# A hybrid decoder block on one core: each mixing program projects the first columns of the next

## The reference

```python
h = rmsnorm(x, mix_norm)
hq, hf, hi, hg, rq, rk, rv, rg, ga, gb = split(h @ w_in)   # 512 x4, 512, 512, 1024, 1024, 1024, 1024
ya = hgrn2_mix(hq, hf, hi, hg, lb, hg_norm)       # 4 heads of 128, chunks of 64
yb = retention_mix(rq, rk, rv, rg, pos, ret_norm) # 4 heads, keys 128, values 256, chunks of 128, rotary
#   in both: o = rmsnorm(per head) * silu(gate)
merged = sigmoid(ga) * (ya @ w_a) + sigmoid(gb) * (yb @ w_b)
x = x + merged @ w_out
x = x + hier_moe(rmsnorm(x))                      # 32 experts, top 1 group, top 2 in it
x = x + sigmoid(rmsnorm(x) @ w_ple_gate) * (p @ w_ple_proj)
return rmsnorm(x)
```

## Time and profile before

| | |
|---|---|
| median of 3 runs | 1540.79 us (1540.4 to 1540.8) |
| the profiled execution | 1540.26 us, its span 1538.4 us |
| PE busy | 1446.3 us, 94% of the span |
| DVE, ACT, POOL busy | 772.2 (50%), 592.4 (39%), 88.6 (6%) us |
| mean granted PE clock | 0.971 of 2.4 GHz |
| DMA | mean 133 GB/s |

### The profile page before, as it was taken

One profiled execution on the slowest core, in us unless ns is written; L12 is line 12 of the kernel. 1 busy time (PEld: TensorE's weight loads), 2 busy tenths in 40 slices (PEclk: granted clock), 3 DMA queues, 4 the chain that ended last, 5 costly groups with the idle time before them and its releaser, 6 DMA issues.

```text
span 1538.4 us, 19246 instructions
## 1 busy us (share of the span) xinstructions
PE 1446.3 (94%) x7882; PEld 1205.3 (78%) x7882; DVE 772.2 (50%) x953; ACT 592.4 (39%) x720; POOL 88.6 (6%) x75
## 2 busy tenths in 40 slices
PE   6999999878997999799999999999699999998997
PEld 5888778667885788588888888988588888876886
DVE  5410366633445543412222224326699999888664
ACT  5310222111112422211111113134488888887555
POOL 0000000000000000000000000000222222221000
PEclk9999999879998999999999999999699999999999
DMA  6200210022213111122222223722699999996221
GB/s 234 83 1 0 61 29 23 7 69 55 55 28 76 35 42 41 43 62 62 61 61 61 61 61 133 265 96 85 259 384 383 391 386 392 375 366 235 107 99 66
DMA packets 103805, 205.23 MB, mean 133 GB/s; under 512 B 12976, under 2 KB 73008, under 8 KB 90160
## 3 DMA queue, kind: packets, MB, share of 16 engines
q1 hardware_dynamic: 93184, 182.89, 33.9%
q0 software_dynamic: 9248, 16.80, 2.9%
q10 hardware_dynamic: 1296, 4.46, 0.7%
HBM read 187.86 MB, written 28.84 MB: 141 GB/s over the span
## 4 chain that ended last, share of the span: by engine, by line
PE 50%; DMA 3%; DVE 2%; ACT 1%; issue 1%; POOLq 0%; DVEq 0%; ACTq 0%; SPq 0%
PE two_banks L174 8%; PE two_banks L176 8%; PE two_banks L175 8%; PE two_banks L2443 4%; PE two_banks L2445 3%; PE two_banks L2444 3%; PE two_banks L2326 2%; PE two_banks L2572 2%; PE two_banks L2328 2%; PE two_banks L2327 2%; PE two_banks L2573 2%; PE two_banks L2574 2%; DMA two_chunk_raw<-w_e 2%; PE two_banks L2433 1%; PE two_banks L2362 1%
## 5 line engine op out<-in xcount | busy, mean ns | idle before, releaser
L1249 DVE TENSOR_TENSOR two_chunk_lo<-two_chunk_raw,two_hi 128x2048 fp32r<-128x2048 f32 x96 | 217.4, 2287 | 24.1 <-ACT two_hi L1245 23.1
L1245 ACT CAST two_hi<-two_chunk_raw 128x2048 fp32r<-128x2048 f32 x96 | 181.4, 1918 | 12.1 <-DMA two_chunk_raw<-w_e 11.7
L221 DVE TENSOR_TENSOR mix_w_lo<-mix_w_raw,mix_w_hi 128x1024 fp32r<-128x1024 f32 (+1 forms) x58 | 66.9, 1160 | 177.7 <-ACT mix_w_hi L217 177.7
L174 PE MATMUL two_banks<-mix_hT_hi,mix_w_hi 128*128 128x512 f32 x256 | 100.5, 392 | 9.9 <-DVE mix_w_lo L221 9.9
L2443 PE MATMUL two_banks<-two_hi,two_xT_hi 128*128 128x512 f32 x256 | 103.3, 404 | 2.3 <-DVE two_xT_lo L1633 1.7
L2445 PE MATMUL two_banks<-two_hi,two_xT_lo 128*128 128x512 f32 x256 | 100.6, 393 | 0.0
L2444 PE MATMUL two_banks<-two_chunk_lo,two_xT_hi 128*128 128x512 f32 x256 | 100.4, 392 | 0.0
L175 PE MATMUL two_banks<-mix_hT_lo,mix_w_hi 128*128 128x512 f32 x256 | 100.3, 392 | 0.0
L176 PE MATMUL two_banks<-mix_hT_hi,mix_w_lo 128*128 128x512 f32 x256 | 100.3, 392 | 0.0
L217 ACT CAST mix_w_hi<-mix_w_raw 128x1024 fp32r<-128x1024 f32 (+1 forms) x58 | 56.8, 985 | 96.4 <-PE two_banks L176 93.2
L174 PE MATMUL gate_gates<-mix_hT_hi,mix_w_hi 128*128 128x512 f32 x192 | 76.4, 398 | 4.9 <-DVE mix_w_lo L221 4.9
(11 more groups left out here) (306 smaller groups left out, 3215.4 us busy)
## 6 DMA issues: line engine op xcount, KB each, us to landing
two_chunk_raw<-w_e SPq DMA_DIRECT2D x102, 1024.0 KB
mix_w_raw<-w_in SPq DMA_DIRECT2D x44, 512.0 KB, 3.8
two_r<-results SPq DMA_DIRECT2D x16, 512.0 KB, 4.5
vals_w_raw<-w_in SPq DMA_DIRECT2D x12, 512.0 KB, 8.2
heads_values<-x SPq DMA_DIRECT2D x8, 512.0 KB, 11.0
reten_swapped<-reten_raw SPq DMA_DIRECT2D x8, 512.0 KB
mix_w_raw<-w_b SPq DMA_DIRECT2D x8, 512.0 KB, 4.7
two_x<-x SPq DMA_DIRECT2D x8, 512.0 KB, 7.5
```

What stands on the lines that cost most here:

```text
L174: nc.tensor.matmul(out, sh, mh, start=(k == 0), stop=False)
L1245: self.nc.scalar.copy(self.high(n)[:], self.raw(n)[:]).then_inc(self.hi_ok, 1)
L1249: self.nc.vector.tensor_tensor(self.low(n)[:], self.raw(n)[:], self.high(n)[:].bitcast(F32), ALU.subtract).then_inc(self.lo_ok, 1)
```

## The change

Each program now also projects the first columns of the one that follows, so that its last head has projections in it as the others do.

- HGRN head 3 projects retention head 0 (eight pieces), into the PSUM tile `sums` that all programs now share; its own outputs go to the tile of the pairs. ACT and DVE split the weights of retention head 1 at its end.
- The retention program begins with the copies of head 0 and the projection of head 1, of which three halves stand ahead of the first transposes. Its ring is numbered from head 1 on. Its last head projects gates 0 and 1 and splits the weights of gates 2 and 3. PE reads the values in place, and GpSimd's copy is gone.
- The squares and sums are taken in the retention: in each head those of two row tiles of the HGRN outputs, and from head 1 on those of the retention head before. The last head's are left to the gate program, in t = 0 and 1, with their own root after t = 2.
- The gate program keeps two gates ahead: turn t, projection t + 2. Projections 12 and 13 are ga and gb of merge tile 0. All loops are written out. ACT's order is silu(t), y_hi(t), high split t + 4.
- The merge starts tile 0 with its branch products.

The diff, cut to its core:

```diff
+            ring.load(sp, HG_HEADS, 0, w_in[:, :, RK:RK + RET_DK])
+            ring.load(sp, HG_HEADS, 1, w_in[:, :, RQ:RQ + RET_DK])
+            ring.ask(sp, 2 * HG_HEADS + 2, first_weights(dram, "reten"), kept["asked"]["reten"])
...
+            def retention_hi(u):
+                act.wait_ge(kept["asked"]["reten"][u], 16)
+                act.wait_ge(projected, 2 * HG_HEADS + u + 1)
+                nc.scalar.copy(ring.hi[:, u], ring.raw[:, u]).then_inc(kept["reten_split"][0], 1)
...
+            def retention_lo(u):
+                dve.wait_ge(kept["reten_split"][0], u + 1)
+                nc.vector.tensor_tensor(ring.lo[:, u], ring.raw[:, u], ring.hi[:, u].bitcast(F32),
+                                        ALU.subtract).then_inc(kept["reten_split"][1], 1)
...
-                    elif i:
-                        pe.wait_ge(out_stored, 2 * i)
-                    pe.wait_ge(state_ok, SU * i + 7)
+                    pe.wait_ge(state_ok, SU * i + 8)
...
-                    if i + 1 < HG_HEADS and n < 8:
+                    if n < 8:
...
+        def parts_of(i):
+
+
+            parts = [(values[:, t, 0:HG_W], mean[:, t, 0:HG_HEADS], HG_DV) for t in range(SUMS * i, SUMS * i + SUMS)]
+            if i:
+                col = HG_W + (i - 1) * RET_DV
+                parts += [(values[:, 2 * g:2 * g + 2, col:col + RET_DV], mean[:, 2 * g:2 * g + 2, HG_HEADS + i - 1], RET_DV)
+                          for g in range(4)]
+            return parts
...
-                if not at(i, RET_HEADS - 1):
-                    ring.load(sp, i + 1, 0, w_in[:, :, bass.ds(RQ + P + i * RET_DK, P)])
-                    ring.load(sp, i + 1, 1, w_in[:, :, bass.ds(RK + P + i * RET_DK, P)])
+                if i + 2 == RET_HEADS:
+                    ring.load(sp, i + 1, 0, w_in[:, :, HGATE:HGATE + P])
+                    ring.load(sp, i + 1, 1, w_in[:, :, HGATE + P:HGATE + 2 * P])
+                if i + 2 < RET_HEADS:
+                    ring.load(sp, i + 1, 0, w_in[:, :, RQ + (i + 2) * RET_DK:RQ + (i + 3) * RET_DK])
+                    ring.load(sp, i + 1, 1, w_in[:, :, RK + (i + 2) * RET_DK:RK + (i + 3) * RET_DK])
                 sp.wait_ge(copied, 2 * i + 2)
-                if not first(i):
+                if i:
                     sp.wait_ge(rot_ok, 2 * i)
...
+                for n, (src, _, _) in enumerate(parts_of(i), parts_before(i)):
+                    if n >= 2:
+                        act.wait_ge(reduced, n - 1)
+                    if n == parts_before(i) + SUMS:
+                        act.wait_ge(out_stored, 4 * i)
+                    to = sq[:, n % 2, :]
+                    nc.scalar.activation(to if len(src.shape) == 2 else to.rearrange("p (t c) -> p t c", t=2), src,
+                                         ACT.Square).then_inc(squared, 1)
                 keys(0)
                 keys(1)
                 for u in range(2):
                     if i + 1 < RET_HEADS:
                         copies(i + 1, u)
-                    if i + 2 < RET_HEADS:
-                        ring.split_hi(act, i + 2, u)
+                        if i + 2 <= RET_HEADS:
+                            ring.split_hi(act, i + 1, u)
+                    else:
+                        act.wait_ge(kept["asked"]["gate"][u], 16)
+                        act.wait_ge(projected, 2 * RET_HEADS - 1 + u)
+                        nc.scalar.copy(ring.hi[:, u], ring.raw[:, u]).then_inc(kept["gate_split"][0], 1)
+                if i + 1 == RET_HEADS:
+                    act.wait_ge(means, 2)
+                    nc.scalar.activation(root[:], mean[:], ACT.Sqrt).then_inc(rooted, 1)
...
+                def reduce():
+                    for n, (_, to, width) in enumerate(parts_of(i), parts_before(i)):
+                        dve.wait_ge(squared, n + 1)
+                        nc.vector.reduce_sum(to, sq[:, n % 2, :].rearrange("p (h c) -> p h c", c=width),
+                                             AX.X).then_inc(reduced, 1)
+
                 if i:
                     dve.wait_ge(out_ok, 4 * i)
                 dve.wait_ge(rot_ok, 2 * i + 1)
                 nc.vector.tensor_tensor(q_in[:].rearrange("p (n c) -> p n c", c=P),
                                         rot[:, 0, :].rearrange("p (n c) -> p n c", c=P),
                                         inter[:, i:i + 1, :].to_broadcast([P, NC, P]), ALU.mult).then_inc(q_in_ok, 1)
+                reduce()
                 score(0)
                 score(1)
-                if i + 2 < RET_HEADS:
-                    ring.split_lo(dve, i + 2, 0)
+                if i + 1 == RET_HEADS:
+                    dve.wait_ge(reduced, parts_before(RET_HEADS))
+                    for cols, width in ((slice(0, HG_HEADS), HG_DV), (slice(HG_HEADS, HEADS - 1), RET_DV)):
+                        nc.vector.tensor_scalar(mean[:, :, cols], mean[:, :, cols], 1.0 / width, EPS,
+                                                ALU.mult, ALU.add).then_inc(means, 1)
+                if i + 1 < RET_HEADS:
+                    ring.split_lo(dve, i + 1, 0)
                 states(0)
                 states(1)
                 if i + 1 < RET_HEADS:
                     by_cos(i + 1)
                 states(2)
-                if i + 2 < RET_HEADS:
-                    ring.split_lo(dve, i + 2, 1)
+                if i + 1 < RET_HEADS:
+                    ring.split_lo(dve, i + 1, 1)
                 states(3)
                 if i + 1 < RET_HEADS:
                     by_sin(i + 1)
+                else:
+                    for u in range(2):
+                        dve.wait_ge(kept["gate_split"][0], u + 1)
+                        nc.vector.tensor_tensor(ring.lo[:, u], ring.raw[:, u], ring.hi[:, u].bitcast(F32),
+                                                ALU.subtract).then_inc(kept["gate_split"][1], 1)
+                    dve.wait_ge(rooted, 1)
+                    nc.vector.reciprocal(rstd[:, :, 0:HEADS - 1], root[:]).then_inc(rstd_ok, 1)
...
-                if i >= RET_HEADS:
-                    return
-                if i and 0 in halves:
+                if 0 in halves:
                     pe.wait_ge(copied, 2 * i - 1 + u)
-                project_block(nc, pe, ring, kept, i, u, sums[:, u], projected, halves)
+                project_block(nc, pe, ring, kept, i - 1, u, sums[:, u], projected, halves)
...
-                project(i + 1, 0, (0,))
+                if i == 0:
+                    project(1, 0)
+                    project(1, 1, (0,))
+                else:
+                    project(i + 1, 0, (0,))
                 keys(0)
                 pair(0)
-                project(i + 1, 0, (1,))
+                if i:
+                    project(i + 1, 0, (1,))
                 keys(1)
                 pair(1)
-                project(i + 1, 1, (0,))
+                if i:
+                    project(i + 1, 1, (0,))
                 updates(0)
                 project(i + 1, 1, (1,))
...
+            def split(t):
+
+                u = t % 2
+                if t < NJ:
+                    ring.split_hi(act, *of_ring(t))
+                elif t < NJ + 2:
+                    act.wait_ge(merge_asked[u], 16)
+                    act.wait_ge(projected, t - 3)
+                    nc.scalar.copy(ring.hi[:, u], ring.raw[:, u]).then_inc(merge_hi, 1)
+                elif t == NJ + 2:
+                    act.wait_ge(merge_asked[u], 32)
+                    act.wait_ge(multiplied, 2)
+                    nc.scalar.copy(ring.hi[:, u, 0:HG_W // P], ring.raw[:, u, 0:HG_W // P]).then_inc(merge_hi, 1)
+
+            for t in range(NJ):
+                if t >= 2:
+                    act.wait_ge(projected, t - 1)
+                if t:
+                    act.wait_ge(y_ok, t)
+                nc.scalar.activation(silu[:], gates[:, t % 2].rearrange("p a b -> p (a b)"), ACT.Silu).then_inc(silu_ok, 1)
+                if t < 2:
+                    square(2 * t)
+                    square(2 * t + 1)
+                act.wait_ge(y_ok, t + 1)
+                nc.scalar.copy(y_hi[:, :, t * P:(t + 1) * P],
+                               y[:].rearrange("p (a b) -> p a b", b=P)).then_inc(hi_ok, 1)
+                if t == 2:
+                    act.wait_ge(means, 1)
+                    nc.scalar.activation(root[:], mean[:], ACT.Sqrt).then_inc(rooted, 1)
+                split(t + 4)
...
+            def turn(t):
+                pe.wait_ge(scaled_ok, t + 1)
+                if t >= 2:
+                    pe.wait_ge(y_ok, t - 1)
+                for j in range(TT):
+                    mm = nc.tensor.transpose(turned[:, t % 2, j, :], scaled[:, j, :], ident[:])
+                mm.then_inc(turned_ok, 1)
+
+            def project(t):
+                pe.wait_ge(silu_ok, t - 1)
+                if t < NJ:
+                    project_block(nc, pe, ring, kept, *of_ring(t), gates[:, t % 2], projected)
+                    return
+                u = t - NJ
+                pe.wait_ge(merge_lo, u + 1)
```

(80 more changed lines are left out.)

244 lines of the change are left out of this document (126 added, 118 removed).

## The result

The changed kernel takes 1525.56 us (median of 4, 1524.36 to 1526.97) where the one before takes 1540.8 (median of 4, 1540.4 to 1542.54): a ratio of 0.9903, 95% interval 0.9891 to 0.9916. That is 15.2 us less; 25.3 were forecast. The profiled execution took 1524.71 us, its span is 1522.8, and the mean granted clock rose from 0.971 to 0.979.

The account below looks back on a forecast made before the run. PE, busy 94% of the span, was taken as the bound, with gains only from its idle time or lower clock. Terms summed along PE moved the first branch product from 676.90 to 651.6, -25.3, giving 1515.5 us, range 1503 to 1527.

Parts of the forecast that it names:

- (a): HGRN head 3, filled with the eight pieces of retention head 0, takes 37.83 us as head 2 does, ending at 331.6.
- (c): Retention start: the rotary chain, not PE, is late by 1.8 us, first transposes at 351.8; bounds 350.0 and 354.
- (d): Retention head 0: 4.6 us from transposes to the last half, 5.7 for that half, second state update at 362.1.
- (e): Retention heads 1 and 2: the swap queued behind a held weight load makes PE wait 3.0 us each, bounds 0 and 5.
- (h): Gate program's start: with silu's table load the joint stays 3.3 us, and gate 2's projection starts at 490.2.
- (i): Gate program: silu queued behind the high split costs 1.44 us a block, 15.4 in all, and a table reload 1.3.
- (j): Merge tile 0 starts with its branch products after a joint of 1.6 us, bounds 0.9 and 4, at 649.1.
- (k): Half clock behind joints and waits costs 2.5 us in all, bounds 0 and 8; the gate program's 1.44 us waits add nothing.
- Rival D: DMA queue: swaps behind weight loads come later still, or the second part loses: + 5 to + 12, 1520 to 1527; chance 0.08.
- C: Gate program: waits for silu drop the clock in part, about 1525 us for half of the eleven, 1534 for all; chance 0.10.
- E: Gate program: each of the eleven waits costs 3.05 us, giving 1549; it decides from 2.3 us a wait on; chance 0.02.
- B: Gate program: ACT's order holds nobody up, because splits find their slot free, giving 1500 us; chance 0.08.

Follow-up runs that it names:

- thin pieces: The changed kernel with 72 of the 96 matmuls of the projection pieces in HGRN head 3 left out: 1519.51 us.
- the longer wait: The changed kernel with one more ScalarE copy of 128x1024 behind the high split in the gate program from block 3 on: 1540.83 us.

## Why the prediction was right in kind, and where it failed

The mechanism and its sign came as written: bare stretches and joints give way, and the two new waits sit where the text put them, behind the releasers that it named. The time missed by 10.1 us, and lies near the upper end of the range; the gain was 15.2 us where 25.3 were forecast. By the steps, with the starts as the two texts give them (HGRN head 3 starts at 293.31, 0.4 us sooner than the 293.68 of the sum):

- (a), (b): right. 37.8 us at clock 1.00, entry 332.1 (ACT), projection 333.20 for 333.6. The thin pieces show that three quarters of the filler cost 9.4 us, and that a quarter of it made the bare head 4 us shorter.
- (c): the chain was late as forecast (351.89 for 351.8). I had called it 1.8 late by the drain of constants and weights, and the swap issued ahead of the weights takes the wait away. Its half clock, 1.0 us, was not in this term.
- (d): right within 0.3 us at full clock. The second state update starts 10.8 us behind the transposes (351.89 to 362.73) where 10.3 were forecast, and 10.0 with the swap first (349.70 to 359.73).
- (e): the named cause was right, both waits too small: 3.93 and 4.44 for 3.0. I took 5.6 us for the hold, up to 1.5 for the weights' data, and gave 3.3 back. Against the order with the swap first the hold was 6.3 us (17.7 less 11.3) and the data 1.8 (8.1 less 6.3); of the sum of both, 8.1, the slack takes 3.2 (additions done at 372.60, transposes at 375.82 with the swap first), and PE was already 1.0 late by half clock: 3.9. Together 2.4 us of the miss, inside my bounds.
- (f), (g): right. The reductions lie under the half projection even when doubled, except in head 0.
- (h): 497.88 for 490.2 is the lateness so far; the joint itself is 3.3 us again (2.21 of waiting and the turn of 1.05).
- (i): right in place and, for the wait, in size: the wait was 1.24 us, the pitch 13.30 for 13.23, one of 14.72 (524.49 to 539.21) for 14.5. The lower clock behind the table load, 1.6 us, was priced at nothing.
- (j): 659.52 less 646.84 is 12.68, a block of 10.9 and 1.8 for the joint: 1.6 was forecast.
- (k): the term that was mis-sized most. Half clock was put at 2.5 us for all joints and waits, bounds 0 and 8. It cost 1.0 + 1.8 + 2.6 in the retention and 1.6 in the gate program, 7.0: 4.5 of the miss. I had a price, the 3.26 us wait that cost 1.7, and put the two waits of 3 and the two joints together at less than two such prices; in the changed kernel all three waits for the keys were followed by half clock, and the two joints (2.02 and 2.21 us) were not.
- After the merge's first product the program took 1522.8 - 659.52 = 863.3 us, 861.5 before. In the seven kernels run after, that part took 861.5 to 864.3 with the same code, so these 1.8 us are not shown to come from the change.

That makes 2.4 + 4.5 + 1.8 = 8.7 of the 9.7 us between forecast and profiled execution; the rest is small differences both ways, the largest the transposes of head 0 (0.5 later, counted from HGRN head 3) and the gate program's distances (0.07 a block for nine blocks). So the range held because its bounds were wide: half clock took 7.0 us of the 8 that (k) allowed, where the sum had 2.5. Rival D had the size (1520 to 1527), but of its mechanism only the term in (e) is there, 2.4 us. C is refuted for the waits of 1.24 us and partly true of one of 2.65. E's point, 2.3 us a wait, was met by the longer wait: its price there is 1.6 three times in seven, not 3.05 each. B is refuted, since silu did wait behind the splits; with silu put first, its premise holds, and the time falls by 18.6 us where B had 15.4.

The Trainium skill (TensorE: Matmul & The Clock Gate, A second HAM failure mode: psum-queue depth-cycling) spoke for C: the clock may swing between its levels when PE idles briefly between groups. The gate program at waits of 2.32 us shows such a swing, and at 1.24 us it shows none. The Trainium skill (ScalarE: Activation LUTs, What ACT_TABLE_LOAD costs) adds a drain to the load. The changed kernel's trace shows none, as before: silu starts 0.02 us behind the end of the 1.28 us load (495.51 to 496.81).

## What to carry to other kernels

When work is moved ahead to fill a bare stretch, its loads and splits move as well, and each now stands in some queue in front of work that used to pass freely: list for every engine what is behind a wait that comes later than before. Two orders of issue, a few lines each, cost 35 of the 50 us that the change is worth without them. The price of a new wait should hold what half clock behind it adds. In these kernels every wait for rotated keys of 2.1 us and more was followed by it, at 1.0 to 3.0 us; those of 2.2 and 2.3 us in the gate program were in 6 of 15 cases, at 1.4 to 1.6 us; the one of 2.65 us behind the table load always, at 1.6; those of 1.24 us never.

## What the runs showed of the hardware

- Half clock behind a wait isn't a function of the wait's length alone. The same joint at the start of the gate program (2.21 us idle, a turn, then the projection) was followed by full clock in the changed kernel (turns 12.1 us apart) and by 0.79 over 8 us where only the swaps were first (turns at 480.90 and 494.61, 13.7 apart). That 1.6 us is why the latter's gain at the merge was 14.4 and not 15.9. Of the eight kernels with this joint, three show the loss: this one, the one with the longer wait (13.5 us between the turns) and the one with thin pieces (13.5). None of the three edits touches the joint.

```profile
481.00:489.00 8.00, 8.00 (x32) 6.38 (x33) 4.83 (x5) 2.99 (x4) 0.00 (x0) 0.79 0.49 134
```

- Small products follow the clock too: a group of eight products of 128x128 took 1.71 us to the next start behind a wait (352.65 to 354.36, granted clock 0.53 from 351.9 to 354.5) and 1.04 at a clock of 1.00 (350.13 to 351.17). The granted clock over a stretch still needn't give the time lost: 0.67 over 5.1 us makes 1.7, and the heads were 1.0 further apart, 0.6 of the difference being a wait that only full clock uncovers.
- With three matmuls in each of eight places, the HGRN head with small products ran at 1.00, where the bare one had 0.68.
- A swap of 1 MB inside SBUF lands 6.3 to 6.4 us after its second issue when nothing is in front, and 8.1 to 8.6 behind 1 MB of weights (heads 1 and 2 of the changed kernel).
